# One encoder step on one core: expert weights loaded by SyncE in an order worked out on the chip, the router's weights waited for at the first routing product

## The reference

```python
x = x + g1 * (merged @ w_out)
h2 = rms_norm(x) * (1.0 + sc2) + sh2
g_logits = t @ w_rg + b_rg                       # t: the rows of h2
e_logits = (t @ w_re + b_re).reshape(-1, N_GROUPS, EXPERTS_PER_GROUP)
# top-1 group, then the top-2 experts inside that group, with weights `combine`
hid = silu(einsum('nd,edf->nef', t, w_gate)) * einsum('nd,edf->nef', t, w_up)
out = einsum('nef,efd->nd', hid * combine[..., None], w_down)
x = x + g2 * out
```

## Time and profile before

| | us |
|---|---|
| median of 3 runs | 1509.81 (1508.29 to 1513.63) |
| profiled execution | 1509.9 |
| its span, first to last instruction | 1508.1 |
| TensorE busy | 1335.0 (89%) |
| VectorE busy | 804.3 (53%) |
| ScalarE busy | 449.2 (30%) |
| mean granted clock of TensorE | 0.942 |

### The profile page before, as it was taken

The page is one execution under the profiler, slowest core; times in us unless marked ns, Lnnn a source line. Parts: engine busy times, 40 slices in busy tenths (PEclk is TensorE's granted clock), DMA queues, the critical chain, the costliest instruction groups (busy, mean ns, idle before and its releaser), DMA issues. The chain is left out here.

```text
span 1508.1 us, 22936 instructions
## 1 busy us (share of the span) xinstructions
PE 1335.0 (89%) x8549; PEld 799.8 (53%) x8550; DVE 804.3 (53%) x1734; ACT 449.2 (30%) x1002; POOL 232.0 (15%) x398
## 2 busy tenths in 40 slices
PE   4999996988989899999968999898997278989995
PEld 3565553656734466666635666563443245555553
DVE  1421123886567878889965656342324633444442
ACT  1521112232254466667134556101112011101110
POOL 0000002003010022221110000000000034545543
PEclk8999998998979999999979999999998589999998
DMA  8500016754031342331031000452323939887651
GB/s 330 188 4 4 32 54 137 233 185 55 11 84 46 95 145 73 98 120 58 30 147 58 2 1 2 149 173 72 112 98 105 332 112 375 304 289 273 218 183 52
DMA packets 138977, 189.97 MB, mean 126 GB/s; under 512 B 31301, under 2 KB 107013, under 8 KB 138661
## 3 DMA queue, kind: packets, MB, share of 16 engines
q1 hardware_dynamic: 105980, 132.56, 27.1%
q0 software_dynamic: 15312, 34.08, 6.7%
q10 hardware_dynamic: 17594, 22.11, 4.4%
HBM read 154.51 MB, written 49.23 MB: 135 GB/s over the span
## 5 line engine op out<-in xcount | busy, mean ns | idle before, releaser
L2311 PE MATMUL ps<-ex_wgu,ex_xT 128*64 (+1 forms) x1408 | 157.5, 382 | 4.9 <-issue 4.0
L1413 DVE TENSOR_SCALAR_CACHE_REDUCE tk_eq<-sc,tk_cand 128x512 bf16<-128x512 f32 (+4 forms) x155 | 146.8, 1007 | 0.0
L2311 PEld LDWEIGHTS ps<-ex_wgu,ex_xT 128*64 128x64 f32 x1408 | 102.2, 138 | 66.8 <-issue 20.6
L1811 PE MATMUL ps<-hT,mergedT 128*128 128x512 f32 (+1 forms) x288 | 120.2, 600 | 4.8 <-DMA op_wr<-in_w_route_expert 4.8
L1347 PE MATMUL ps<-zT,gt_w 128*128 128x352 f32 (+1 forms) x384 | 120.9, 468 | 0.0
L1347 PE MATMUL ps<-hT,gt_w 128*128 128x352 f32 (+1 forms) x336 | 105.8, 468 | 0.0
L1347 PEld LDWEIGHTS ps<-zT,gt_w 128*128 128x128 f32 x384 | 73.0, 190 | 44.1
L1811 PEld LDWEIGHTS ps<-hT,mergedT 128*128 128x128 f32 (+1 forms) x288 | 50.9, 186 | 68.4 <-issue 62.8
L1376 ACT ACTIVATE mask<-sc,tk_cand 128x384 bf16<-128x384 f32 (+1 forms) x62 | 82.3, 1329 | 14.7 <-DVE tk_cand L1429 14.7
L1347 PEld LDWEIGHTS ps<-hT,gt_w 128*128 128x128 f32 x336 | 63.8, 190 | 38.5
L2324 PE MATMUL ps<-ex_wd,ex_hidT 128*64 x352 | 82.1, 609 | 0.0
(11 more groups left out here) (489 smaller groups left out, 2236.7 us busy)
## 6 DMA issues: line engine op xcount, KB each, us to landing
ex_wgu<-in_w_gate SPq DMA_DIRECT2D x10, 1024.0 KB, 7.5
ex_wgu<-in_w_up SPq DMA_DIRECT2D x10, 1024.0 KB, 12.5
ex_wd<-in_w_down SPq DMA_DIRECT2D x10, 1024.0 KB, 11.9
sp_ada_w<-in_w_ada SPq DMA_DIRECT2D x9, 1024.0 KB
ex_wgu<-in_w_gate ACTq DMA_DIRECT2D x6, 1024.0 KB, 5.8
ex_wgu<-in_w_up ACTq DMA_DIRECT2D x6, 1024.0 KB, 11.7
ex_wd<-in_w_down ACTq DMA_DIRECT2D x6, 1024.0 KB, 11.8
merge_left_dram<-qiT SPq DMA_DIRECT2D x8, 544.0 KB, 6.3
```

Of the source, the lines that this page charges most:

```text
L1413: return v.tensor_scalar(junk[j], m.sc[0:r, c:c + w], scalar, 0.0, op, ALU.add, accum_out=cnt[0:r, j:j + 1])
L1811: i = nc.tensor.matmul(m.ps[rows, 2 * (t % 2) + n, :], m.mergedT[:, k, t * P:t * P + r], m.wout[:, k, n * 512:(n + 1) * 512], start=k == 0 ...
L2311: i = nc.tensor.matmul(m.ps[mine, 2 + h, 0:FD], xT[:, k, mine], w[side][:, k, :, P * h:P * (h + 1)], start=k == 0, stop=k == KD - 1)
```

## The change

The wait for the router's weights moves from the head of TensorE's projection block to its first routing product. SyncE issues all later expert loads, one after another, in the order in which the places come free on either side; VectorE works that order out (`m.order`: expert, place, tile count that frees the place) and with it the count of landed loads that each tile needs (`tile_ready`). ScalarE issues none and has one loop over all tiles; TensorE reads one register less at an expert. The waits that hold a load (`gp` for gate and up, `dn` for down) stay.

```diff
+LATER = NE - 2 * RING
...
                     if t:
                         pe.wait_ge(lc, t)
+                    else:
+                        pe.wait_ge(wl, 32)
+                        pe.wait_ge(one, 4)
...
-                pe.wait_ge(wl, 32)
-                pe.wait_ge(one, 4)
...
+def load_gate_up(engine, m, A, e, place, sem):
+
+    for n, x in enumerate((A.w_gate[e], A.w_up[e])):
+        engine.dma_start(m.wgu[:, place, :, FD * n:FD * (n + 1)].rearrange("p o k n -> p (o k) n"),
+                         x.rearrange("o (k p) n -> p (o k) n", p=P)).then_inc(sem, 16)
...
+                for side in range(2):
+                    for j in range(RING, NE // 2):
+                        at = LATER // 2 * side + j - RING
+                        i = nc.gpsimd.memset(source[:, at:at + 1], float(NE * (RING * side + j % RING) + expert_at(side, j)))
+                i.then_inc(io, 1)
...
+                step(tt(before[:, :, :], bc(done[:, 0:n], 2, n), bc(done[:, half:half + n], 1, n), ALU.is_gt))
+                step(v.tensor_reduce(turn[:, 0:n], before[:, :, :], AX.X, ALU.add))
...
+                step(tt(cmp[:, :, :], cmp[:, :, :], bc(more[:, :, :].rearrange("p s j -> p (s j)"), 1, MAXT), ALU.mult))
...
-                weights_here(0)
-                for j in range(RING, EACH):
-                    weights_here(j - RING + 1)
-                    used = end_of(sp, 0, j - RING)
+                for i in range(2 * RING):
+                    weights_here(m.wl[i], 48)
+                for i in range(LATER):
+                    if i:
+                        weights_here(later[(i - 1) % 2], 48 * ((i - 1) // 2 + 1))
+                    e = sp.value_load(m.order[0:1, 0, i:i + 1], min_val=0, max_val=NE - 1)
+                    place = sp.value_load(m.order[0:1, 1, i:i + 1], min_val=0, max_val=2 * RING - 1)
+                    used = sp.value_load(m.order[0:1, 2, i:i + 1], min_val=1, max_val=MAXT)
                     sp.wait_ge(gp, 2 * used)
-                    load_gate_up(sp, m, A, 0, j)
+                    load_gate_up(sp, m, A, bass.ds(e, 1), bass.ds(place, 1), later[i % 2])
                     sp.wait_ge(dn, used)
-                    load_down(sp, m, A, 0, j)
+                    load_down(sp, m, A, bass.ds(e, 1), bass.ds(place, 1), later[i % 2])
...
-                expert_by_expert(pe, tile, ahead=lambda j: pe.wait_ge(m.wl[1][j % RING], 48 * (j // RING + 1)))
+                start = 0
+                for j in range(EACH):
+                    end = pe.value_load(m.expert_done[0:1, EACH + j:EACH + j + 1], min_val=j + 1, max_val=MAXT)
+                    with pe.Fori(start, end) as n:
+                        tile(n, j)
+                    start = end
...
-                expert_by_expert(act, tile, behind=next_weights)
+                tiles = act.value_load(m.expert_done[0:1, NE - 1:NE], min_val=EACH, max_val=MAXT)
+                with act.Fori(0, tiles) as n:
+                    tile(n)
```

More of the change, by code:

```diff
@@ L1944, in expert_at, with load_down @@
     return EPG * SIDES[side][j % 2] + j // 2
[L1947 to L1958, removed]
+def load_gate_up(engine, m, A, e, place, sem):
+    for n, x in enumerate((A.w_gate[e], A.w_up[e])):
+        engine.dma_start(m.wgu[:, place, :, FD * n:FD * (n + 1)].rearrange("p o k n -> p (o k) n"),
+                         x.rearrange("o (k p) n -> p (o k) n", p=P)).then_inc(sem, 16)
+def load_down(engine, m, A, e, place, sem):
+    engine.dma_start(m.wd[:, place, :, :].rearrange("p o k n -> p (o k) n"),
+                     A.w_down[e].rearrange("o (k p) n -> p (o k) n", p=P)).then_inc(sem, 16)
 def routing(nc, m, A):
@@ L1981, in routing @@
         code = sb("rt_code", [P, 2, TILES])
+        source = sb("rt_source", [P, LATER])
+        turn = sb("rt_turn", [P, LATER])
+        before = sb("rt_before", [P, LATER // 2, LATER // 2])
+        is_turn = sb("rt_is_turn", [P, LATER, LATER])
+        order = sb("rt_order", [P, LATER])
+        orderi = sb("rt_order_int", [P, LATER], I32)
+        ready, more = sb("rt_ready", [P, 2, NE // 2]), sb("rt_more", [P, 2, NE // 2])
         at = sb("rt_at", [P, 2, 2 * TILES], I32)
@@ L2001, in _ @@
                     for side in range(2):
-                        load_gate_up(sp, m, A, side, j)
-                        load_down(sp, m, A, side, j)
+                        e, place = (slice(x, x + 1) for x in (expert_at(side, j), RING * side + j))
+                        sem = m.wl[2 * j + side]
+                        load_gate_up(sp, m, A, e, place, sem)
+                        load_down(sp, m, A, e, place, sem)
             @block.gpsimd
@@ L2123, in _ @@
                 step(v.tensor_reduce(te[:, 0, :], cmp[:, :, 0:half], AX.X, ALU.add))
-                step(ts(m.tile_ready[:, :], te[:, 0, :], float(half - 1), 1.0, ALU.min, ALU.add))
-                step(ts(m.tile_place[:, :], m.tile_ready[:, :], -1.0, None, ALU.add))
+                step(ts(m.tile_place[:, :], te[:, 0, :], float(half - 1), None, ALU.min))
                 step(ts(m.tile_place[:, :], m.tile_place[:, :], 1, None, ALU.bitwise_and))
                 step(v.tensor_copy(m.expert_done[:, :], done))
+                n = LATER // 2
@@ new lines, in _ @@
+                step(tt(before[:, :, :], bc(done[:, 0:n], 2, n), bc(done[:, half:half + n], 1, n), ALU.is_gt))
+                step(v.tensor_reduce(turn[:, 0:n], before[:, :, :], AX.X, ALU.add))
+                step(v.tensor_reduce(turn[:, n:], before[:, :, :].rearrange("p a b -> p b a"), AX.X, ALU.add))
+                step(ts(turn[:, n:], turn[:, n:], -1.0, float(n), ALU.mult, ALU.add))
+                turns = turn[:, :].rearrange("p (s j) -> p s j", s=2)
+                step(tt(turns, turns, bc(iota[:, 0:n], 1, 2), ALU.add))
@@ new lines, in _ @@
+                step(ts(ready[:, :, RING:], turns, 2 * RING + 1.0, None, ALU.add))
+                for side in range(2):
+                    for j in range(RING):
+                        step(v.memset(ready[:, side, j:j + 1], 2.0 * j + side + 1.0))
+                step(tt(cmp[:, :, half:], bc(iota[:, 0:MAXT], 2, half), bc(done[:, half:], 1, MAXT), ALU.is_ge))
+                step(tt(more[:, :, 0:half - 1], ready[:, :, 1:half], ready[:, :, 0:half - 1], ALU.subtract))
+                step(v.memset(more[:, :, half - 1:], 0.0))
@@ new lines, in _ @@
+                step(tt(cmp[:, :, :], cmp[:, :, :], bc(more[:, :, :].rearrange("p s j -> p (s j)"), 1, MAXT), ALU.mult))
+                by_side = te[:, 1:3, :].rearrange("p s n -> p n s")
+                step(v.tensor_reduce(by_side, cmp[:, :, :].rearrange("p n (s j) -> p n s j", s=2), AX.X, ALU.add))
+                step(ts(te[:, 2, :], te[:, 2, :], 1.0, None, ALU.add))
+                step(tt(te[:, 1, :], te[:, 1, :], te[:, 2, :], ALU.max))
+                step(ts(m.tile_ready[:, :], te[:, 1, :], 1.0, None, ALU.add))
@@ new lines, in _ @@
+                step(tt(is_turn[:, :, :], bc(turn[:, :], 1, LATER), bc(iota[:, 0:LATER], 2, LATER), ALU.is_equal))
+                for side in range(2):
+                    mine = slice(n * side, n * (side + 1))
+                    step(v.scalar_tensor_tensor(source[:, mine], done[:, half * side:half * side + n], float(4 * NE), source[:, mine],
+                                                ALU.mult, ALU.add))
+                step(tt(is_turn[:, :, :], is_turn[:, :, :], bc(source[:, :], 1, LATER), ALU.mult))
@@ new lines, in _ @@
+                step(v.tensor_reduce(order[:, :], is_turn[:, :, :], AX.X, ALU.add))
+                step(v.tensor_copy(orderi[:, :], order[:, :]))
+                step(ts(m.order[:, 0, :], orderi[:, :], NE - 1, None, ALU.bitwise_and))
+                step(ts(m.order[:, 1, :], orderi[:, :], 4, None, ALU.logical_shift_right))
+                step(ts(m.order[:, 1, :], m.order[:, 1, :], 3, None, ALU.bitwise_and))
+                step(ts(m.order[:, 2, :], orderi[:, :], 6, None, ALU.logical_shift_right))
@@ L2171, in experts @@
         place_of = (slice(0, HALF), slice(HALF, P))
+        later = [m.sem(f"ex_later_loaded{i}") for i in range(2)]
         def wait(engine, sem, value):
@@ L2191, in run @@
             after(engine.value_load(m.loops[0:1, 1:2], min_val=LOOPS[0] - 1, max_val=LOOPS[1] - 1))
[L2193 to L2207, removed]
         def previous(step, i, b):
@@ L2218, in _, with weights_here @@
             def _(sp):
-                def weights_here(j):
-                    sp.wait_ge(m.wl[0][j % RING], 48 * (j // RING + 1))
+                def weights_here(sem, value):
+                    sp.wait_ge(sem, value)
                     sp.sem_inc(here, 1)
-                weights_here(0)
-                for j in range(RING, EACH):
-                    weights_here(j - RING + 1)
-                    used = end_of(sp, 0, j - RING)
+                for i in range(2 * RING):
[6 more added lines that the diff above has]
+                    used = sp.value_load(m.order[0:1, 2, i:i + 1], min_val=1, max_val=MAXT)
```

(12 more changed lines are left out.)

9 lines of the change are left out of this document (2 added, 7 removed).

## The result

The changed kernel takes 1501.76 us (median of seven runs, 1499.24 to 1504.77); the kernel before takes 1509.81 (seven runs, 1508.29 to 1515.75). The ratio is 0.9942, 95% interval 0.9926 to 0.9958: 8.0 us faster.

What follows compares the result with a forecast made beforehand. The expert stage was taken to run at TensorE's product rate, with ScalarE issue stalls and weights that can become late; 1509.9 - 3.05 (router wait) + 1.3 (VectorE) - 6.8 (experts) = 1501.4 us, range 1494 to 1509.

Steps and rivals of the forecast that it cites:

- the likeliest case: Expert stage: one weight load takes 13 to 14.6 us, giving 1497.4 to 1505.0 us; chance 0.56.
- the router term: Output projection: without the wait for the router's weights TensorE starts 3.05 us earlier; 0 to 1.7 us extra from the clock.
- the experts' term: Expert stage: the stall passes to the weights, tile 9 itself gains 5.0 us, three expert changes 1.8; together 6.8 us.
- VectorE: Routing stage: 7.2 us of added instructions, 5.88 us of them under an existing wait, put 1.3 us on the path.
- ScalarE: Expert stage: its two long weight issues vanish; reloading the activation table every tile, 1.28 us, is hidden.
- L: Expert stage: time of one weight load from first issue to landing, taken as 14.0 us; 0.5 us moves the time by 3.
- h: SyncE's queue: handoff from one load's landing to the next load's start, with three register loads, taken as 2.0 us.
- A: Expert stage: weights are never late, a load taking at most 12.1 us; 1495.2 us, or 1493.5 with the clock; chance 0.17.
- B: Expert stage: loads wait longer at the gathers, 15 us each, tile 9 starts 6 us later; same time, 1507.4 us; chance 0.17.
- C: Expert stage: the serial queue becomes the bound at 17.3 us a load, tile 12 waits 23 us; slower, 1524.4 us; chance 0.10.

Runs made afterwards that it cites:

- the loads alone: Changed kernel with the router wait put back ahead of the first projection product, against the kernel before: 1505.98 us, ratio 0.9974.
- half the bytes: Changed kernel whose twelve later loads each bring half of the rows of their three matrices: 1493.41 us in one run.
- the first experiment: Kernel before with only the router wait moved to the first routing product: 1508.16 us, ratio 0.9981 against the kernel before.

## Why the prediction was right

**The time.** 1501.4 was forecast and 1501.76 measured, inside the likeliest case's own range. The mechanism is the forecast one; that the sum is so close is in part luck. In the traces the router term was 1.4 us too small for its stage and the experts' term 2.8 to 4.9 us too large, and single executions begin the projection up to 4.6 us apart.

**The router wait**, -3.05. The lead was 4.47 us in the profile: the idle fell from 4.82 to 1.72, which is the 3.05 (3.10), and the clock that fell to 0.50 before stayed at 1.00. Those are the 0 to 1.7 us that the prediction left in its range; it took the lower end on the strength of an idle of 1.7 us elsewhere that was followed by 0.51, and that row was not a guide for this place, where all seven traces kept 1.00. So the term was 1.4 us too small for its stage. At the end this part by itself was worth 2.2 us at the median, 0.6 to 5.1 by the interval: how much of the stage's 4.5 us arrives there stays open.

**VectorE**, +1.3. Measured 26.99 - 25.46 = 1.53. The wide reduction took 0.85 (0.86 was taken), a 144-element one 0.31 (0.34 was taken); the wait of 5.88 us is gone, as forecast.

**ScalarE.** No issue of it is in the chain. Its table load in every tile is hidden: it still waited 198.2 us for TensorE's products, in 44 waits. The view of waits, changed kernel:

```profile
ACT ex_silu L2393 <- PE ps L2344: 198.2, 44, 11.1
...
PE ps L2344 <- SPq L2251: 7.7, 3, 4.1
```

**The experts**, -6.8. The mechanism came as forecast, in place and order: the stall goes from ScalarE's queue to the weights, at tiles 4, 5 and 9, with idle times of 3.03, 4.11 and 0.52 us (1 to 4, and about 1, were named); the gates of loads 1 to 6 are 16.6 us apart (16 were named); tile 9 itself gives 5.17 (5.0) and the expert changes 1.68 (1.8). What was mis-sized, for this execution, is L: 14.56 instead of 14.0, and h 2.13 instead of 2.0. Six loads and five handoffs make 6 x 0.56 + 5 x 0.13 = 4.0 us, and tile 9, counted from tile 1, starts 4.95 us later than before, where about 0.4 was forecast (1332.2 against 1331.82). In this execution the experts therefore give only 4.95 - 5.17 - 1.68 = -1.9 us. In the trace of the loads alone they give 4.0 us: its gates are 16.0 us apart, as forecast, and tile 9 starts 2.75 us later than before. So the loads do differ among executions of the same queue, by 2.2 us at tile 9. By the medians the loads with the longer routing are worth 4.4 us, so the loads alone about 4.4 + 1.5 = 5.9; the interval of that run makes this 3.8 to 7.1, in which the forecast lies.

Half clock after the waits at tiles 4 and 5 (1.7 and 1.5 us of slower products) was not foreseen. It cost nothing here: the chain runs through SyncE's landings alone from 1239.97 to 1333.21, and tile 9 would only have waited longer. In the trace of the loads alone it did cost time: the chain goes over from load 3's landing to TensorE at tile 5, whose slow products (8.81 us) are in it, and no later load holds TensorE up.

**The rivals.** A's time was right for weights that are never late (1493.4 with half the bytes), but not its condition. The page "DMA: Bandwidth & Descriptors" of the Trainium skill (Anatomy of one DMA) would put a load at 9.2 us, an estimate by its 2.0 us and 436 GB/s, a fit that the page gives for one DMA issued by GpSimd, not for SyncE's. The trace does not agree, with 11.4 to 16.6 us for a load that shares the engines with the gathers. B came close in the profiled execution: load 6 lands at 1333.21 - 1227.88 = 105.3 us after tile 1's start, where the forecast has 1332.2 - 1231.08 = 101.1 and B 107.1; L was less than B's 15 there, and h more than 2.0. The first eight gates, of which the forecast says 16 us apart and B 17, are 16.7 apart in it and 16.3 in the trace of the loads alone. C did not happen: no wait for weights stands after tile 9.

The Trainium skill, on the page "DMA: Bandwidth & Descriptors" (Issuing engines are not separate DMA queues), calls the issue time that a second engine saves usually small beside the DMA; here the long issues were the price of the second engine, 9.42 us beside another load and 0.75 with that load cut down.

## What to carry to other kernels

When a queue with a stall is merged into another, work out when each load lands, not only what the queue costs: the stall moves to the loads, and the time between a landing and the next issue is paid once per load in the row, as far as the loads do not get shorter by it. Read registers and do address arithmetic ahead of the wait, and keep a second load in flight; these two edits were worth as much again as the whole change (1501.8 to 1492.8 us). A change that shortens an idle time early in the kernel should be timed by itself and read in more than one trace: here the stage's own gain was the same in all (about 4.5 us), while tile 0 took from 13.1 to 14.75 us and blurred it.

## What the runs showed of the hardware

- Whether an idle TensorE was followed by a granted clock of 1.2 GHz (0.50) could not be told from the length of the idle alone, but one place behaved alike in every trace: 1.72 or 1.73 us ahead of the projection was followed by 1.00 in all seven traces that have it, 4.8 us there by 0.50 to 0.58 in the other three. An idle of about 1.7 us elsewhere was followed by 0.51, one of 2.00 us ahead of tile 5 by slow products (8.81 us, the loads alone); after ScalarE's first stall (3.63 us idle before, 4.04 in the first experiment) the clock stayed at 1.00 in the one and fell to 0.50 in the other.
- The issue of one 1 MB transfer took 0.37 to 9.8 us on its queue; on ScalarE's, what made it long was a load of SyncE in the engines (9.42 us, and 0.75 with that load cut down). On SyncE, where nothing is queued behind it but the wait for its own landing, an issue of 4.50 us (at 1269.90, changed kernel) lies inside the 14.16 us that this part of the load takes.
- A register read from a table costs SyncE about 0.57 us, in two pieces of 0.28 and 0.16 with gaps (the two rows of line 2258 in the chain of the changed kernel). Three of them were 1.7 us of every handoff, though the table had been there since the routing.
